# Scores of two heads given in turn from the two halves of the array's rows, and the modulation product in the eighth PSUM bank

## The reference, cut to what matters

```python
def swa_latent(q, k, v, k_ctx, v_ctx, sink):
    ...
        s_loc = jnp.einsum('bqgrd,bkgd->bgrqk', q_b, k_b).astype(jnp.float32) * SWA_SCALE
        s_loc = jnp.where(valid, s_loc, -jnp.inf)
        s_ctx = jnp.einsum('bqgrd,bcgd->bgrqc', q_b, k_ctx).astype(jnp.float32) * SWA_SCALE
        p = sink_softmax(jnp.concatenate([s_ctx, s_loc], axis=-1), sink).astype(v.dtype)
        return (jnp.einsum('bgrqc,bcgd->bqgrd', p[..., :n_ctx], v_ctx)
                + jnp.einsum('bgrqk,bkgd->bqgrd', p[..., n_ctx:], v_b))

def hybrid_layer(xl, xc, c, c_ctx, ...):
    sh1, sc1, g1, sh2, sc2, g2 = jnp.split((jax.nn.silu(c) @ ada_w + ada_b)[:, None, :], N_MOD, axis=-1)
    ...
    xl = xl + g1 * (jnp.concatenate([a_l, b_l, cv_l], axis=-1) @ w_o)
    xl = xl + g2 * ec_ffn(rmsnorm(xl, norm2_g) * (1 + sc2) + sh2, router_w, w_gate, w_up, w_down)
```

## Time and profile before

| | |
|---|---|
| time, median of 3 runs | 2189.89 us (2189.32 to 2190.16) |
| the profiled execution | 2189.6 us, its span 2187.8 us |
| mean granted TensorE clock | 0.982 of full |
| PE busy | 2040.3 us (93%) |
| PEld busy | 1589.6 us (73%) |
| DVE busy | 922.2 us (42%) |
| ACT busy | 451.7 us (21%) |
| POOL busy | 89.0 us (4%) |
| DMA | 435.70 MB, mean 199 GB/s |

### The profile page before, as it was taken

One profiled execution on the slowest core, in us unless ns is written; L12 is line 12 of the kernel. 1 busy time (PEld: TensorE's weight loads), 2 busy tenths in 40 slices (PEclk: granted clock), 3 DMA queues, 4 the chain that ended last, 5 costly groups with the idle time before them and its releaser, 6 DMA issues.

```text
span 2187.8 us, 32669 instructions
## 1 busy us (share of the span) xinstructions
PE 2040.3 (93%) x14109; PEld 1589.6 (73%) x14109; DVE 922.2 (42%) x1888; ACT 451.7 (21%) x993; POOL 89.0 (4%) x89
## 2 busy tenths in 40 slices
PE   6999999999899997669999999999999998999998
PEld 3444586655565575447878878999987888889998
DVE  2137723232337531214454414566325543246662
ACT  3004512111223421001332112100013411210001
POOL 1000010000010000000001100000100011000000
PEclk9999999999999999889999999999999999999999
DMA  9751537999933479996333124455552331344462
GB/s 370 252 194 45 197 137 283 387 425 426 412 117 141 164 288 425 423 424 248 117 115 116 39 95 144 153 186 145 164 173 78 116 116 39 113 146 162 138 175 76
DMA packets 182145, 435.70 MB, mean 199 GB/s; under 512 B 6346, under 2 KB 72818, under 8 KB 166130
## 3 DMA queue, kind: packets, MB, share of 16 engines
q1 hardware_dynamic: 180864, 431.19, 53.4%
q10 hardware_dynamic: 1138, 2.41, 0.3%
HBM read 432.53 MB, written 1.05 MB: 198 GB/s over the span
## 4 chain that ended last, share of the span: by engine, by line
PE 82%; DMA 11%; DVE 4%; issue 1%; ACT 1%; ACTq 0%; DVEq 0%
PE bank L284 77%; DMA ring<-in_exp_w_up 5%; DMA ring<-in_exp_w_gate 2%; PE bank L620 2%; DMA ring<-in_exp_w_down 1%; PE bank L889 1%; DMA cst<-in_exp_w_up 1%; DMA ring<-in_w_in 1%; PE bank L1053 1%; DMA arena<-in_x 1%; DVE arena L838 0%; DVE arena L943 0%; ACT arena L843 0%; PE bank L541 0%; PE bank L1566 0%
## 5 line engine op out<-in xcount | busy, mean ns | idle before, releaser
L284 PE MATMUL bank<-h,ring 128*128 128x256 f32 (+2 forms) x3296 | 722.7, 377 | 8.6 <-DMA ring<-in_w_in 2.2
L284 PEld LDWEIGHTS bank<-h,ring 128*128 128x128 f32 x3296 | 579.5, 191 | 133.7 <-issue 60.2
L284 PE MATMUL bank<-arena 128*128 128x128 f32 (+11 forms) x3528 | 454.1, 325 | 45.4 <-DMA arena<-in_exp_w_up 11.3
L284 PEld LDWEIGHTS bank<-arena 128*128 128x128 f32 (+5 forms) x3528 | 343.6, 170 | 133.6 <-issue 53.8
L284 PE MATMUL bank<-arena,ring 128*128 128x128 f32 (+1 forms) x1704 | 267.9, 317 | 1.0 <-PE bank L284 1.0
L284 PEld LDWEIGHTS bank<-arena,ring 128*128 128x128 f32 x1704 | 245.9, 191 | 19.6 <-PE bank L284 1.8
L843 ACT ACTIVATE arena<-bank 128x256 f32<-128x256 f32 (+6 forms) x225 | 99.8, 463 | 496.9 <-PE bank L284 474.1
L284 PE MATMUL bank<-ring,arena 128*32 128x128 f32 (+1 forms) x1600 | 123.2, 355 | 28.5 <-DMA ring<-in_exp_w_up 16.5
L838 DVE COPY arena<-bank 128x512 f32<-128x512 f32 (+6 forms) x88 | 49.9, 569 | 211.1 <-PE bank L284 144.8
L284 PEld LDWEIGHTS bank<-ring,arena 128*32 128x32 f32 (+1 forms) x1600 | 86.1, 134 | 67.7 <-DMA ring<-in_exp_w_up 21.3
L687 POOL TENSOR_TENSOR arena<-arena 128x256 f32<-128x256 f32 (+1 forms) x53 | 46.5, 877 | 1437.0 <-ACT arena L674 1205.1
(11 more groups left out here) (377 smaller groups left out, 1725.0 us busy)
## 6 DMA issues: line engine op xcount, KB each, us to landing
ring<-in_w_in SPq DMA_DIRECT2D x32, 2048.0 KB, 7.9
ring<-in_exp_w_up SPq DMA_DIRECT2D x21, 2048.0 KB, 14.9
ring<-in_ada_w SPq DMA_DIRECT2D x18, 2048.0 KB, 10.2
ring<-in_exp_w_gate SPq DMA_DIRECT2D x16, 2048.0 KB, 13.9
ring<-in_exp_w_down SPq DMA_DIRECT2D x16, 2048.0 KB, 16.0
ring<-in_w_ffn_gate SPq DMA_DIRECT2D x10, 2048.0 KB, 7.8
ring<-in_w_ffn_up SPq DMA_DIRECT2D x10, 2048.0 KB, 7.9
arena<-in_exp_w_down SPq DMA_DIRECT2D x9, 2048.0 KB, 17.5
```

Source lines behind the costliest of these rows:

```text
L284: return PE.matmul(o, lhsT, rhs, start=(k == 0), stop=(k == n - 1))
```

## The change

Two edits. The product `mods` now always has bank 7, which the rows product before it used and which ACT has copied by then. And `attend_tensor` gets a function `paired`: for the heads of 64 rows in the first block (i modulo 12 is 6 or more) the call for the even head takes four banks, two for each of the two heads, and then gives the four products in turn, even head, odd head, even head, odd head; the call for the odd head does nothing. The attention of the second block calls without it and is unchanged.

```diff
-            elif key[0] == "mods_rows":
+            elif key[0] in ("mods_rows", "mods"):
                 b = 7
...
-        def attend_tensor(pe, heads, prob, probT, tag, between=None):
+        def attend_tensor(pe, heads, prob, probT, tag, between=None, paired=lambda i: False):
...
             def scores(i):
-                q, keys, nk = heads[i][0:3]
+                if paired(i) and i % 2:
+                    return
+                group = (i, i + 1) if paired(i) else (i,)
+                places = [[take(pe, "scores", tag, hd, j) for j in range(2)] for hd in group]
                 for j in range(2):
-                    b = take(pe, "scores", tag, i, j)
-                    mm(b[:, 0:nk], q(j), keys, 0, 1).then_inc(*tensor.mark("scores", tag, i, j))
+                    for hd, b in zip(group, places):
+                        q, keys, nk = heads[hd][0:3]
+                        mm(b[j][:, 0:nk], q(j), keys, 0, 1).then_inc(*tensor.mark("scores", tag, hd, j))
...
-            attend_tensor(pe, all_heads(l), prob1, probT1, ("heads", l), ada)
+            attend_tensor(pe, all_heads(l), prob1, probT1, ("heads", l), ada, lambda i: i % 12 >= 6)
```

## The result

The changed kernel takes 2201.29 us in the median (2200.57 to 2203.67, four runs) against 2189.61 us (2183.32 to 2190.16, four runs) before: ratio 1.0066, interval 1.0054 to 1.0079. It is 12 us slower; 2194.1 was forecast, with a range up to 2197.5. The profiled execution took 2201.95 us, its span 2200.2.

A forecast was written before the change was run, and what follows sets the result against it. PE was taken to bound the kernel, with DVE nearly full too in masked attention pairs. Terms 1.3 + 0.3 + 0.5 + 2.1 + 0 = 4.2 us, plus 0.3, on 2189.6 gave 2194.1 us; range 2190.5 to 2197.5.

The forecast's parts named there:

- The loop: Masked pair in layer 0's attention: a cycle through PE, DVE and ACT takes 8.68 us against 8.01, 0.67 us more.
- the routing: Layer 0's expert routing: the rows product waits for ACT's copy of the token transposes out of bank 7, 2.1 us later.
- the bank shift: Behind attention: with the modulation product in bank 7 the turn advances less, so all later banks move; 2.1 us in layer 0.
- the exit from layer 0's masked half: Lone head 12 after the masked pairs: 0.48 us of product behind the wait; head 10's transposes 1.3 us late.
- The scores themselves: Attention pairs: two heads' scores cost what one costs, so a masked pair takes 1.92 us instead of 3.84.
- the new wait: Masked pairs: heads 8 and 9's scores wait for head 7's second exponential on ACT, leaving PE idle 2.8 us a pair.
- Layer 0 at full clock: Layer 0's attention: 1.3 us later from the masked half and 0.3 us from three unmasked pairs.
- The unmasked half: Layer 0's unmasked pairs: 6.3 us against 6.16, 0.3 us for three pairs.
- Layer 1: Layer 1's attention, six masked heads: 0.5 us more, chosen between bounds of 0 and 1.3.
- The second block: Second block's gates: a 0.81 us wait for DVE's reciprocal moves from layer 0 to layer 1; net 0, bounds -1 and +1.
- Rival 4: Thinner attention stages: granted clock falls to 1.2 GHz for one stretch, some 3 us more, 2197 us; chance 7%.

## Why the prediction was wrong

The loop, the routing and the bank shift came out as worked out. What failed is the clock, which the prediction left out of its sum and held as a rival at 7%; a smaller miss is the exit from layer 0's masked half.

- **The scores themselves: right.** Two heads on two halves cost what one costs: scores and attended product of a pair are 3.79 us at full clock, 3.80 in the prediction.
- **The loop: right.** 8.68 us was worked out, 8.85 and 8.90 were measured with the products at full clock, and the new wait binds in each pair. The second wait, 1.02 us ahead of the odd head's transposes, was not named; it is part of the idle time that was forecast.
- **Layer 0 at full clock: 2.80 us measured, 1.3 + 0.3 forecast.** The unmasked half is 6.39 a pair, as worked out. The mis-sized term is the exit: from head 8's transposes to head 10's I had 7.24 us (229.92 to 237.16), the kernel with idle matmuls has 8.01 (229.50 to 237.51). Head 12's first product waits as long as its second, so both (1.03 us) stand behind the wait, not 0.48, and the wait ends 5.10 us behind the transposes, not 4.88. The small steps of each loop add the rest.
- **The routing: right.** 2.22 us measured, 2.1 forecast, by the mechanism named.
- **Layer 1: right at full clock** (0.45 us in both profiles with idle matmuls there, 0.5 forecast). The 0.5 was a choice between bounds of 0 and 1.3, so that it fits so well is luck in part.
- **The second block: right.** The gate's wait of 0.81 us moved from layer 0 to layer 1, to 1891.89 us in the changed kernel's profile.
- **The clock: the step that failed.** Rival 4 held the cause, "the granted clock falls in the thinner stages", at 7% and 3 us "for one stretch", from a row that shows full clock at 15.95 of 20 us busy. Measured: 10.93 - 2.80 = 8.1 us in layer 0, 4.64 - 0.45 = 4.2 us in layer 1, and 0.9 in the routing (2.85 against 1.92), 13.2 in all. Of these, 1.6 in layer 0 and 2.6 in layer 1 lie behind waits for DVE that the kernel before has too; its own profile happened to show full clock at both. Behind the new waits there are 6.5 + 1.6 + 0.9 = 9.0 us, against the 3 of the rival and the nothing of the sum. Two errors are in it. One row with the clock up was read as a rule for all stretches like it, when it was one execution: at that row's own wait of 2.10 us the clock fell in four of six profiles. And the price was taken once, although the wait comes back with every pair, and the fall with most of them.
- **The sum of it.** At full clock 2.80 + 2.22 + 0.45 = 5.5 us, and 13.2 for the clock, on the 2189.6 of the profiled execution give 2208.3. The profiled execution took 2201.95: 1.3 us less lie ahead of layer 0's attention, 4.6 behind that of layer 1 and 0.4 between, all within what single executions differ by.

The wait for the exponentials that I had found is thus the cause of most of the loss: at full clock it costs some 3 us, and it leaves the holes in PE's work in which the clock falls. The routing's wait adds 2.2 us.

## What to carry to other kernels

When an edit leaves TensorE waiting in a loop, price the idle time that the new order leaves at both clocks, and for every turn of the loop. One profile with the clock up does not show that it stays up: look at the same place in several. Before pairing products for an overlap, look at who held the banks: taking a group's banks all at once makes the first product wait for the last holder, and here layer 0's attention lost 2.8 us at full clock with pairs on banks in turn, and gained 1.2 with the masked pairs alone, on banks given by hand. Where banks go in turn, one take less shifts every bank behind it, and a stage far from the edit can get a wait (2.2 us here) that the diff does not show.

## What the runs showed of the hardware

The clock fell although no wait of PE was longer than 1.69 us in the masked half, and in stretches where PE was busy 7.79 of 10.50 us (6.15 of 8.85 in a pair whose products ran at full clock). The Trainium skill warns in TensorE: Matmul & The Clock Gate, Why this matters for your kernels, of idle gaps longer than any in these pairs; in these traces it also fell behind shorter ones that come back with every pair. The section A second HAM failure mode: psum-queue depth-cycling of the same page of the Trainium skill describes such a case in bf16: short idle times of PE between groups of products, with banks cycled, make the clock go to and fro. The trace agrees for fp32, with 0.84 of the clock over a pair.

The fall is not a property of the code alone. The product behind the wait of 2.10 us in layer 1 ran in 1.95 us in one kernel's profile and in 3.40 in another's, with the same instructions and waits around it. Behind the wait of 1.64 or 1.65 us in layer 0 that all kernels have, it was slow in two of thirteen profiles; behind the 2.0 to 2.1 us of layer 1, in nine of eleven without idle matmuls. What decides it was not tested here, nor whether the length of a wait counts or the share of time that PE is busy.

Idle matmuls bought time: 7.5 us of products that nobody reads, three times 1.03 and 1.46, came with a masked half and exit of layer 0 6.5 us shorter than in the changed kernel's first profile. It is a cure for the clock only; it does not bring the loop under 8.85 us.
